# New orders for the calls of the four compute engines in a layer of window attention and retention, and one wait in its group norm

## The reference

```python
h = rms_norm(x, norm_gain)
proj = jnp.einsum('bsd,de->bse', h, w_in)          # 1024 -> 5632 columns
aq, ak, av, ag, rq, rk, rv, rg = jnp.split(proj, SPLIT_POINTS, axis=-1)
attn = window_attention(aq, ak, av, q_norm_gain, k_norm_gain, sink_logits)
ret = retention(rq, rk, rv, ret_norm_gain)
mixed = jnp.concatenate([attn * silu(ag), ret * silu(rg)], axis=-1)
x = x + jnp.einsum('bse,ed->bsd', mixed, w_out)    # 2048 -> 1024 columns
```

## Time and profile before

| | us |
|---|---|
| median of 3 runs | 1573.88 |
| lowest and highest | 1573.47, 1574.04 |
| the profiled execution, first to last instruction | 1571.6 |
| TensorE busy in it | 1552.0 |
| VectorE busy | 1124.6 |
| ScalarE busy | 833.3 |
| GpSimd busy | 457.9 |

### The profile page before, as it was taken

The page is one execution under the profiler, slowest core; times in us unless marked ns, Lnnn a source line. Parts: engine busy times, 40 slices in busy tenths (PEclk is TensorE's granted clock), DMA queues, the critical chain, the costliest instruction groups (busy, mean ns, idle before and its releaser), DMA issues.

```text
span 1571.6 us, 24771 instructions
## 1 busy us (share of the span) xinstructions
PE 1552.0 (99%) x8120; PEld 1355.1 (86%) x8120; DVE 1124.6 (72%) x2874; ACT 833.3 (53%) x2331; POOL 457.9 (29%) x453
## 2 busy tenths in 40 slices
PE   6999999999999999999999999999999999999999
PEld 5898888988889888898988989889898898988887
DVE  7899587797856757577875766757687574775864
ACT  6766565655535445464654645446464454635641
POOL 6565657553322021120302212121120211202210
PEclk9999999999999999999999999999999999999999
DMA  8888485755775444463655635526447455344451
GB/s 319 308 287 310 155 334 215 269 210 212 296 258 197 161 177 183 165 236 125 215 206 208 250 140 186 211 97 249 172 158 281 146 207 191 140 191 137 174 212 54
DMA packets 123327, 323.65 MB, mean 206 GB/s; under 512 B 16832, under 2 KB 60224, under 8 KB 123200
## 3 DMA queue, kind: packets, MB, share of 16 engines
q1 hardware_dynamic: 122240, 320.50, 55.6%
q10 hardware_dynamic: 960, 1.57, 0.3%
HBM read 250.72 MB, written 71.30 MB: 205 GB/s over the span
## 4 chain that ended last, share of the span: by engine, by line
PE 92%; DVE 4%; POOL 1%; DMA 1%; issue 1%; ACT 1%; SPq 0%; DVEq 0%; ACTq 0%; POOLq 0%
PE jb L1469 26%; PE jb L1470 26%; PE jb L1471 26%; PE ob L1528 2%; PE s L1504 2%; PE ptb L1513 2%; PE ob L1488 1%; PE s L1567 1%; PE ab L1578 1%; PE s L1566 1%; POOL wL L396 1%; PE s L1405 1%; DMA stage<-wp_dram 1%; PE ab L1405 0%; PE ab L1407 0%
## 5 line engine op out<-in xcount | busy, mean ns | idle before, releaser
L1469 PE MATMUL jb<-wH,hTH 128*128 128x512 f32 (+1 forms) x1024 | 376.3, 367 | 13.0 <-POOL wL L396 10.7
L1470 PE MATMUL jb<-wL,hTH 128*128 128x512 f32 (+1 forms) x1024 | 372.6, 364 | 0.0
L1471 PE MATMUL jb<-wH,hTL 128*128 128x512 f32 (+1 forms) x1024 | 372.3, 364 | 0.0
L1469 PEld LDWEIGHTS jb<-wH,hTH 128*128 128x128 f32 x1024 | 193.0, 188 | 33.6 <-POOL wL L396 12.4
L1471 PEld LDWEIGHTS jb<-wH,hTL 128*128 128x128 f32 x1024 | 193.1, 189 | 20.4
L1470 PEld LDWEIGHTS jb<-wL,hTH 128*128 128x128 f32 x1024 | 193.3, 189 | 17.9
L1469 PE MATMUL jb<-wH,mxH 128*128 128x512 f32 x512 | 207.1, 405 | 0.9 <-ACT rawqn L550 0.6
L1469 PE MATMUL jb<-hTH,wH 128*128 128x512 f32 x512 | 201.4, 393 | 0.0
L1471 PE MATMUL jb<-wH,mxL 128*128 128x512 f32 x512 | 200.6, 392 | 0.0
L1470 PE MATMUL jb<-wL,mxH 128*128 128x512 f32 x512 | 200.5, 392 | 0.0
L1470 PE MATMUL jb<-hTL,wH 128*128 128x512 f32 x512 | 200.0, 391 | 0.0
(11 more groups left out here) (145 smaller groups left out, 3011.6 us busy)
## 6 DMA issues: line engine op xcount, KB each, us to landing
wH<-scrH SPq DMA_DIRECT2D x144, 512.0 KB, 7.0
wL<-scrL SPq DMA_DIRECT2D x144, 512.0 KB, 7.9
stage<-wp_dram SPq DMA_DIRECT2D x48, 512.0 KB, 6.7
scrH<-wH SPq DMA_DIRECT2D x48, 512.0 KB, 6.9
scrL<-wL SPq DMA_DIRECT2D x48, 512.0 KB, 7.8
wH<-scrH SPq DMA_DIRECT2D x48, 384.0 KB, 5.4
wL<-scrL SPq DMA_DIRECT2D x48, 384.0 KB, 6.6
out_dram<-acc SPq DMA_DIRECT2D x16, 512.0 KB, 3.0
```

The costliest lines, as they stand in the source:

```text
L1469: pe.matmul(o, lh, rh_, start=i == 0, stop=False)
L1470: pe.matmul(o, lh, rl_, start=False, stop=False)
L1471: m = pe.matmul(o, ll, rh_, start=False, stop=i == last)
```

## The change

The four lists of calls, on TensorE, VectorE, ScalarE and GpSimd, are replaced by other orders of the same calls (772, 1471, 1089 and 432 of them), drawn up by a list scheduler that gives the call with the longest remaining way precedence. gnv has one wait more, so that mv is not written before gnm has read it. SyncE's queue, the order of the jobs among themselves and every operation are as before. In the excerpt the lines are those around the first calls, around the seam of units 8 and 9, and gnv; the order is ScalarE's start and seam, gnv, VectorE's seam, TensorE's start and seam:

```diff
-            xh(0, 0, 0); wh1(0, 0, 0); wh1(0, 0, 1); xh(0, 0, 1); wh1(0, 0, 2); wh1(0, 0, 3); xh(0, 0, 2)
...
+            rh(0, 0); wh1(0, 0, 0); wh1(0, 0, 1); wh1(0, 0, 2); xh(0, 0, 0); wh1(0, 0, 3); wh1(0, 0, 4); xh(0, 0, 1)
...
-            qkv(9, 0); kwh_ah(8, 3); ocopy(8, 2); rh(8, 3); v_shift(9, 0); mth(8, 0); qkv(9, 1); gnx(8, 2)
-            v_shift(9, 1); qkv(9, 2); xsq(3, 0); ocopy(8, 3); v_shift(9, 2); tqh(9, 0); mth(8, 1); xsq(3, 1)
...
+            ocopy(8, 2); mth(8, 0); qkv(9, 1); gnx(8, 2); tqh(9, 0); ocopy(8, 3); mth(8, 1); v_shift(9, 0)
...
             def gnv(n, t):
+                if 4 * n + t:
+                    v.wait_ge(S["s_nb"], 4 * n + t)
                 for h in range(2):
                     i = v.bn_aggr(mv[:, h], st[:, h])
                 link(i)
...
-            mtl(8, 0); carry_in(9); gnm(8, 2); qk_stats(9, 1); v_parts(9, 1); gnb(8, 2); qk_norm(9, 1)
-            rupd(8, 3); qk_stats(9, 2); v_parts(9, 2); gna(8, 3); gnv(8, 3); qk_norm(9, 2); tql(9, 0); mtl(8, 1)
...
+            qk_norm(9, 1); gna(8, 3); mtl(8, 1); gnv(8, 3); part1(9, 0); tql(9, 1); qk_stats(9, 2); gnm(8, 3)
...
-            S_(0, 0); job(0, 6); TQ(0, 2); S_(0, 1); job(0, 7); TQ(0, 3); S_(0, 2); PT(0, 0); job(0, 8)
-            PT(0, 1); S_(0, 3); PV(0, 0); job(0, 9); A(0, 0); PT(0, 2); job(0, 10); PV(0, 1); I(0, 0); A(0, 1)
...
-            job(9, 0); I(8, 2); MT(8, 0); job(9, 1); job(9, 2); I(8, 3); TQ(9, 0); MT(8, 1); job(9, 3)
-            job(8, 12); TQ(9, 1); job(8, 13); S_(9, 0); MT(8, 2); job(8, 14); TQ(9, 2); job(8, 15); S_(9, 1)
...
+            job(0, 0); job(0, 1); job(0, 2); TQ(0, 0); job(0, 3); S_(0, 0); job(0, 4); XB(0); job(0, 5); TQ(0, 1)
+            job(0, 6); TQ(0, 2); S_(0, 1); PT(0, 0); job(0, 7); TQ(0, 3); S_(0, 2); PT(0, 1); A(0, 0); job(0, 8)
...
+            job(8, 10); A(8, 2); I(8, 1); job(8, 11); A(8, 3); I(8, 2); job(9, 0); MT(8, 0); job(9, 1); I(8, 3)
+            MT(8, 1); TQ(9, 0); job(9, 2); TQ(9, 1); S_(9, 0); MT(8, 2); job(9, 3); S_(9, 1); job(8, 12); PT(9, 0)
```

More of the change, by code:

```diff
@@ L449, in _ @@
[L449 to L481, removed]
@@ new lines, in _ @@
+            mix(0, 3); rupd(0, 1); kwl_al(0, 2); gna(0, 1); rl(0, 2); kw_am(0, 3); gnb(0, 0); gnv(0, 1); rupd(0, 2)
+            rvg(0, 3); kwl_al(0, 3); gnm(0, 1); rl(0, 3); gna(0, 2); gnb(0, 1); mtl(0, 0); qk_stats(1, 0); gnv(0, 2)
+            rupd(0, 3); qk_stats(1, 1); mtl(0, 1); gna(0, 3); qk_norm(1, 0); gnm(0, 2); v_parts(1, 0); gnv(0, 3)
+            qk_norm(1, 1); gnb(0, 2); gnm(0, 3); v_parts(1, 1); rl(1, 0); tql(1, 0); qk_stats(1, 2); v_parts(1, 2)
+            xms_(1, 0); gnb(0, 3); xms_(1, 1); qk_norm(1, 2); part1(1, 0); tql(1, 1); mtl(0, 2); add(0, 0)
@@ new lines, in _ @@
+            gna(4, 2); mtl(4, 0); gnv(4, 2); gnm(4, 2); rupd(4, 3); qk_stats(5, 0); gnb(4, 2); mtl(4, 1); gna(4, 3)
+            qk_norm(5, 0); gnv(4, 3); v_parts(5, 0); rl(5, 0); gnm(4, 3); qk_stats(5, 1); v_parts(5, 1); tql(5, 0)
+            qk_norm(5, 1); gnb(4, 3); mtl(4, 2); part1(5, 0); tql(5, 1); qk_stats(5, 2); v_parts(5, 2); xms_(2, 0)
+            part2(5, 0); part1(5, 1); qk_norm(5, 2); add(4, 0); ptl(5, 0); qk_stats(5, 3); part2(5, 1); add(4, 1)
+            qk_norm(5, 3); tql(5, 2); mtl(4, 3); add(4, 2); v_parts(5, 3); xms_(2, 1); add(4, 3); part1(5, 2)
@@ new lines, in _ @@
+            rupd(5, 2); kwl_al(5, 3); rl(5, 3); qk_stats(6, 0); gna(5, 2); mtl(5, 0); gnv(5, 2); qk_norm(6, 0)
+            v_parts(6, 0); gnm(5, 2); rupd(5, 3); qk_stats(6, 1); gnb(5, 2); v_parts(6, 1); tql(6, 0); qk_norm(6, 1)
+            gna(5, 3); mtl(5, 1); gnv(5, 3); part1(6, 0); tql(6, 1); qk_stats(6, 2); gnm(5, 3); mtl(5, 2); part2(6, 0)
+            part1(6, 1); gnb(5, 3); qk_norm(6, 2); ptl(6, 0); add(5, 0); part2(6, 1); qk_stats(6, 3); add(5, 1)
+            tql(6, 2); qk_norm(6, 3); add(5, 2); mtl(5, 3); v_parts(6, 2); v_parts(6, 3); rl(6, 0); xms_(2, 2)
@@ new lines, in _ @@
+            gnm(6, 1); gnb(6, 1); kw_am(6, 3); rvg(6, 3); rupd(6, 2); kwl_al(6, 3); rl(6, 3); qk_stats(7, 0)
+            gna(6, 2); mtl(6, 0); gnv(6, 2); qk_norm(7, 0); v_parts(7, 0); gnm(6, 2); rupd(6, 3); qk_stats(7, 1)
+            gnb(6, 2); v_parts(7, 1); tql(7, 0); qk_norm(7, 1); gna(6, 3); mtl(6, 1); gnv(6, 3); part1(7, 0)
+            qk_stats(7, 2); gnm(6, 3); tql(7, 1); mtl(6, 2); qk_norm(7, 2); part2(7, 0); gnb(6, 3); qk_stats(7, 3)
+            v_parts(7, 2); add(6, 0); mtl(6, 3); part1(7, 1); tql(7, 2); qk_norm(7, 3); ptl(7, 0); part2(7, 1)
@@ new lines, in _ @@
+            v_parts(13, 0); gnm(12, 2); rupd(12, 3); qk_stats(13, 1); gnb(12, 2); v_parts(13, 1); tql(13, 0)
+            qk_norm(13, 1); gna(12, 3); mtl(12, 1); gnv(12, 3); part1(13, 0); tql(13, 1); qk_stats(13, 2); gnm(12, 3)
+            mtl(12, 2); part2(13, 0); gnb(12, 3); qk_norm(13, 2); part1(13, 1); qk_stats(13, 3); tql(13, 2)
+            ptl(13, 0); qk_norm(13, 3); part2(13, 1); add(12, 0); mtl(12, 3); add(12, 1); v_parts(13, 2); part1(13, 2)
+            tql(13, 3); add(12, 2); v_parts(13, 3); add(12, 3); part2(13, 2); add(12, 4); part1(13, 3); ptl(13, 1)
```

882 lines of the change are left out of this document (413 added, 469 removed).

## The result

The changed kernel takes 1603.86 us (median of 4 runs, 1602.99 to 1605.24) where the kernel before takes 1573.68 (1573.47 to 1574.04): a ratio of 1.0192 with a 95% interval of 1.0178 to 1.0207. That is 25.0 us above the forecast and 17.9 us above the top of the range.

What follows compares the result with a forecast made beforehand. TensorE, busy for nearly the whole span, was taken as the bound. Start -1.5, seam +5.5 and units 1 to 4 +1.0 made +5.0 us on 1573.9: 1578.9 us, range 1570.0 to 1586.0, likeliest 1576 to 1582.

Steps and rivals of the forecast that it cites:

- What bounds the kernel: Whole program: TensorE busy 1552.0 of 1571.6 us; from 150 to 1450 us the old order has nothing left to give.
- Part 1, the wait: gnv on VectorE, 63 calls: wait already met when reached; 1.3 to 2.5 us of VectorE time, counting only where VectorE is late.
- Part 2, TensorE's groups cost the same anywhere: Small TensorE groups moved to other gaps between jobs: cost nothing, with 1 us to either side over the program.
- Part 3, the start: First units, to about 150 us: gains and new stalls sum to -1.5 us, bounds -5 and +2.
- The hidden rows: Start, VectorE's chain for job(0,1): runs beside an idle GpSimd after wl1 ends earlier, -1.3 us.
- S_(0,0): Start, group moved up between job(0,3) and job(0,4): waits for its tile's keys, +1.2 us, bounds nothing and 1.5.
- A(0,0): Start, group now behind job(0,7) and three groups: stalls TensorE for 1.4 us, waiting for GpSimd's rkL near 58 us.
- The old stalls from 50 to 150 us: TensorE's idle time in that stretch of the old order, 2.8 us, may go: -2.8 us.
- Part 4, the seam: Between two units, eleven times from unit 5: TensorE's MT waits for VectorE's mtl, 0.5 us a unit, +5.5 us, bounds 0 and +11.
- Part 5, units 1 to 4: Units where ScalarE and GpSimd also split weights: looser seam but fuller VectorE, +1 us for the four, bounds -0.5 and +4.
- Rival C: Much slower: seam costs 1 us in each unit, units 1 to 4 lose 3 us; 1586.4 us, chance 0.17 (above 1582).

Runs made afterwards that it cites:

- the two zero-fill runs: Old order and new order, each with GpSimd's wl1 filling its target with zeros instead of subtracting (low weight halves left out): 1570.38 and 1570.54 us.

## Why the prediction was wrong

**What bounds the kernel.** Right as a reading, wrong as a conclusion. TensorE had 1300 of 1300 us, but I did not read how far ahead of TensorE the other engines were, and that is what the new order spends. Taken from the two zero-fill runs (the start of each TensorE group, less the end of the last thing it needs): of the 28 to 31 groups in each of units 1, 2 and 3, the closest stands 1.2, 1.4 and 1.4 us behind in the old order and 0.25, 0.15 and 0.3 us in the new one; closer than 1 us are 0, 0 and 0 against 9, 6 and 5. MT(1,3) is one of them. VectorE's mtl and TensorE's MT in the old order, then in the new one, both with the fill:

```profile
216.99 0.41 DVE L909 TENSOR_TENSOR mxL<-ab,mxH 128x256 fp32r<-128x256 f32 x1
...
219.56 0.38 PE L1577 MATMUL ab<-ident,oraw 128*128 128x128 f32 x2
```
```profile
210.30 0.42 DVE L836 TENSOR_TENSOR mxL<-ab,mxH 128x256 fp32r<-128x256 f32 x1
...
210.86 0.41 PE L1472 MATMUL ab<-ident,oraw 128*128 128x128 f32 x2
```

2.16 us (219.56 less 217.40) against 0.14 (210.86 less 210.72). One block of wl1 lasts 1.37 us. The old order has VectorE drawn out just as much: from 150 to 490 us VectorE is busy for 256.67 us, and for 227.19 with the fill, 29.5 us less, while TensorE is busy for all 340 us in both (windows of the kernel before, then of the old order with the fill). Operation by operation (each against the median of the same operation behind 600 us, where no wl1 runs), VectorE loses 46.3 us in units 1 to 4 of the kernel before and 46.7 in the kernel after (6.9 and 4.8 with the zero fill); 51 and 57 operations are drawn out by over 0.3 us. The old order does not avoid the blocks; it absorbs them, though not by much: with the subtraction in place, its closest groups in units 2 and 3 stand 0.8 us behind what they need.

```profile
150.00:490.00 340.00, 340.00 (x1800) 297.74 (x1799) 256.67 (x619) 189.97 (x507) 159.62 (x149) 1.00 0.65 241
```
```profile
150.00:490.00 340.00, 340.00 (x1803) 298.01 (x1802) 227.19 (x624) 189.25 (x507) 103.06 (x148) 1.00 0.65 240
```

**Part 1, the wait: right.** 0, and 1.0001 was measured. That run has the old order, where gnm stands at least five places ahead of the gnv that waits for it; in the new order it is at least two. There the zero-fill runs bound it, as the new order with the wait ends 0.2 us from the old one without it.

**Part 2, TensorE's groups cost the same anywhere: right, but for the clock.** What I left out is that a stall of TensorE can be followed by a stretch at the 1.2 GHz level. It had no term in my sum, and it cost up to 6.8 us. Behind its first wait the old order has no stall above 1.9 us, and no such stretch.

**Part 3, the start: wrong, -1.5 against +7.7 in unit 0.** The hidden rows do come earlier, some 2 us for the second job. S_(0,0) waits (the 2.6 us of L1399 above; I took 1.2, and at most 1.5), and A(0,0) waits 3.0 us (I took 1.4). There the step that failed was laying rk and rkl end to end "with about 0.05 us between each two". The lists show two wh1 calls ahead of rk and two wl1 calls ahead of rkl, and the trace has them there. ScalarE, then GpSimd, in the kernel after:

```profile
59.62 1.14 ACT L500 ACTIVATE wH<-stage 128x512 fp32r<-128x512 f32 x2
60.66 0.57 ACT L593 ACTIVATE kr<-jb 128x512 f32<-128x512 f32 x1
...
60.37 2.89 POOL L385 TENSOR_TENSOR wL<-stage,wH 128x512 fp32r<-128x512 f32 x2 [1.28 <-ACT wH L500]
63.23 1.26 POOL L405 TENSOR_TENSOR rkL<-kr,rkH 128x512 fp32r<-128x512 f32 x1
```

That was to be had before the run. The old stalls from 50 to 150 us (2.8 us) did go, as none of their waits is left in that stretch; but new ones of 8.8 us came in their place. The stretches at the 1.2 GHz level behind S_(0,0) and A(0,0), up to 3.4 us, had no term either.

**Part 4, the seam: right in place and kind, +5.5 against +3.1.** S_ and the MT behind it in unit 9 of the kernel after, with VectorE's mtl:

```profile
913.22 0.72 PE L1399 MATMUL s<-kHL,qS 128*128 128x256 f32 x4
913.98 0.41 PE L1473 MATMUL ab<-ident,oraw 128*128 128x128 f32 x2
...
913.40 0.42 DVE L837 TENSOR_TENSOR mxL<-ab,mxH 128x256 fp32r<-128x256 f32 x1
```

MT(8,2) starts 0.76 us behind S_(9,0) and 0.16 us behind the end of mtl. An S_ takes 0.47 to 0.56 us where nothing holds the next call, so the loss is some 0.23 us in each of eight units, and it is some 0.6 at S_(n,1) in units 8 and 12: 8 x 0.23 + 2 x 0.63 = 3.1, an estimate. That it meets the 3.1 us measured from unit 5 on is in part luck, since unit 5, which is not in it, takes 0.9 us more and the last unit 0.8 less. The term of 0.5 a unit was oversized by 0.2 to 0.3, within the error that I named.

**Part 5, units 1 to 4: the step that made the miss, +1 against +20.0.** Its sentence said that "VectorE is fuller and its operations are drawn out beside wl1" and then gave this 1 us, with no working. Rival C had the mechanism, "the lock would also have to fall on qk_norm and gna", and priced it at 3 us. It did fall on qk_norm (716 ns on average against 512) and on part1 and part2, but never on gna: its addition takes 406 to 423 ns in all 64 calls. The cost per hit was in the earlier trace rows: 786 ns on an xg. What I did not do is lay out one seam of unit 2 as I did for unit 9, with one block of wl1 in it; with 0.1 to 0.3 us to spare and 1.3 us for a block, four hits a unit that are not absorbed give 5 us (an estimate). Measured were 4.7, 7.3, 4.8 and 3.2 us in units 1 to 4.

**What stays open.** The closest few groups of the old order stand 1.2 to 1.8 us behind with the fill, and blocks of 2.4 us cost it only 1.3 us from 150 to 490 us. The margin of a single group does not settle it: a block must also meet that group's own chain, and how much of the old order's safety is margin and how much is where the blocks fall was not told apart. Taking a single engine's list from the old order was not tried.

## What to carry to other kernels

A bound engine that is busy for all of a stretch tells nothing of how close its helpers are; before reordering, work out for each of its instructions the distance to what it needs, and compare the smallest ones with the longest single instruction that can block a helper. The list scheduler used up those distances here. It would have to take the operations that another engine can draw out at their drawn-out length, or keep a margin of one block; no run tried either. Cutting the blocking instruction in two won back 12 of 30 us in the new order and cost nothing in the old one. Cutting it in four cost more than it gave: each part has some 0.2 us of its own (an estimate from 1373, 794 and 498 ns for 512, 256 and 128 columns), and GpSimd came late.
